# An expert down product in one fp32 pass per operand, or in three products of split operands

## The reference

```
scores = sigmoid(xt @ router_w)                 # 512 x 64, top 8 of 64 experts per token
...
def expert_block(args):                         # one block: up to 128 rows of one expert
    tok, e = args
    xb = xt[tok]                                # 128 x 1024
    h = silu(xb @ w_gate[e]) * (xb @ w_up[e])   # 128 x 256
    return h @ w_down[e]                        # 256 x 1024 weights, result 128 x 1024
...
routed = segment_sum(y * row_gate, row_tok)
```

## Time and profile before

| what | value |
|---|---|
| median of three executions | 2637.62 us (2608.13 to 2641.20) |
| the profiled execution's own time | 2625.82 us |
| its span, first to last instruction | 2623.9 us |
| busy: PE, DVE, ACT, POOL | 89%, 65%, 41%, 30% of the span |
| TensorE clock granted, mean | 0.947 of full speed |
| DMA, mean over the span | 226 GB/s |

### The profile page before, as it was taken

One profiled execution on the slowest core, in us unless ns is written; L12 is line 12 of the kernel. 1 busy time (PEld: TensorE's weight loads), 2 busy tenths in 40 slices (PEclk: granted clock), 3 DMA queues, 4 the chain that ended last, 5 costly groups with the idle time before them and its releaser, 6 DMA issues.

```text
span 2623.9 us, 35527 instructions
## 1 busy us (share of the span) xinstructions
PE 2323.8 (89%) x9437; PEld 1630.5 (62%) x9437; DVE 1695.1 (65%) x1753; ACT 1070.3 (41%) x1199; POOL 783.7 (30%) x682
## 2 busy tenths in 40 slices
PE   7652997899999999869999999798999999999995
PEld 4220455666666666647988888554666666666663
DVE  5998455666666667553257788545666666666665
ACT  2334014455555555422233333202455555555552
POOL 3663022444434434320000000002334443444432
PEclk9885989999999999988999999899999999999997
DMA  6110137999999999943232222232899999999995
GB/s 205 42 54 0 35 126 240 334 341 362 356 356 333 332 342 352 318 152 112 89 89 65 81 80 71 85 109 86 284 340 354 358 343 337 327 357 340 337 348 163
DMA packets 189297, 592.57 MB, mean 226 GB/s; under 512 B 18781, under 2 KB 88453, under 8 KB 153908
## 3 DMA queue, kind: packets, MB, share of 16 engines
q1 hardware_dynamic: 165140, 517.92, 54.1%
q0 software_dynamic: 24096, 73.88, 12.0%
HBM read 547.11 MB, written 51.38 MB: 228 GB/s over the span
## 4 chain that ended last, share of the span: by engine, by line
PE 35%; DMA 27%; DVE 12%; POOLq 11%; issue 9%; POOL 4%; ACT 1%; SPq 0%; DVEq 0%; ACTq 0%
DMA acc<-BIG,IDXS 22%; PE PS L1455 10%; POOLq L546 9%; DVE BIG L1084 6%; PE PS L1439 5%; PE PS L1237 4%; DMA BIG<-xrows,IDXG 3%; PE PS L1367 3%; PE PS L1346 3%; PE PS L1271 2%; POOL IDXS L586 2%; DMA W<-in_exp_w_up 2%; POOL IDXG L572 1%; PE PS L1468 1%; PE PS L1493 1%
## 5 line engine op out<-in xcount | busy, mean ns | idle before, releaser
L995 DVE TENSOR_TENSOR WL<-W,WH 128x2048 fp32r<-128x2048 f32 x276 | 627.9, 2291 | 276.6 <-ACT WH L691 276.0
L691 ACT ACTIVATE WH<-W 128x2048 fp32r<-128x2048 f32 x276 | 523.0, 1911 | 127.0 <-DMA W<-in_exp_w_up 118.0
L1367 PE MATMUL PS<-W,BIG 128*128 128x512 f32 x1104 | 510.6, 606 | 2.0 <-DVE BIG L1007 2.0
L1346 PE MATMUL PS<-WH,XH 128*128 128x512 f32 x1104 | 443.5, 402 | 5.8 <-DVE XL L988 5.5
L1346 PE MATMUL PS<-WH,XL 128*128 128x512 f32 x1104 | 432.2, 391 | 0.0
L1346 PE MATMUL PS<-WL,XH 128*128 128x512 f32 x1104 | 430.3, 390 | 0.0
L595 POOL DMA_INDIRECT acc<-BIG,IDXS x138 | 304.1, 2204 | 313.4 <-issue 295.3
L1367 PEld LDWEIGHTS PS<-W,BIG 128*128 128x128 f32 x1104 | 205.1, 196 | 209.3 <-issue 206.7
L1346 PEld LDWEIGHTS PS<-WH,XH 128*128 128x128 f32 x1104 | 208.1, 189 | 48.4 <-issue 8.7
L1346 PEld LDWEIGHTS PS<-WH,XL 128*128 128x128 f32 x1104 | 207.5, 188 | 45.2
L1346 PEld LDWEIGHTS PS<-WL,XH 128*128 128x128 f32 x1104 | 208.3, 189 | 39.2
(11 more groups left out here) (233 smaller groups left out, 3174.4 us busy)
## 6 DMA issues: line engine op xcount, KB each, us to landing
W<-in_exp_w_gate SPq DMA_DIRECT2D x138, 1024.0 KB, 8.1
W<-in_exp_w_up SPq DMA_DIRECT2D x138, 1024.0 KB, 11.3
W<-in_exp_w_down SPq DMA_DIRECT2D x138, 1024.0 KB, 7.0
RAW<-in_w_kv SPq DMA_DIRECT2D x48, 512.0 KB, 3.8
RAW<-in_attn_w_q SPq DMA_DIRECT2D x24, 512.0 KB, 3.7
W<-in_conv_w_in SPq DMA_DIRECT2D x8, 1024.0 KB, 11.4
acc<-BIG SPq DMA_DIRECT2D x9, 512.0 KB, 3.7
W<-in_conv_w_out SPq DMA_DIRECT2D x4, 1024.0 KB, 6.6
```

What stands on the lines that cost most here:

```text
L691: A(WH[:, s, c, :], W[:, 3 * s + c, :], ACT.Copy).then_inc(s_wh[l], 1)
L995: v.tensor_tensor(WL[s][:, c, :], W[:, 3 * s + c, :], WH[:, s, c, :].bitcast(F32), ALU.subtract).then_inc(s_wl[l], 1)
L1346: last = mm(PS[:, 3 + s, :].rearrange("p (a b) -> p a b", a=2), a, w, start=(k == 0 and i == 0), stop=(k == KT - 1 and i == 2))
L1367: last = mm(PS[:, 5 + h, :], HTm[:, s, k * P:(k + 1) * P], wd[:, k, h * 512:(h + 1) * 512], start=(k == 0), stop=(k == 1))
```

## The change

The down product is made as the gate and up products are: from a high and a low part of each operand, in three fp32r products (12 matmul calls of 512 columns per block instead of 4 float32 calls).

- ACT copies the down weights to a new buffer WDH as fp32r (`down_high(b+1)`, 128x2048), between `weights_high(b+2)` and `silu(b+1)`. It copies the transposed hidden rows to HTH (`hidden_high(b)`) at the start of its step, and it copies both halves of the output (`out(b)`).
- DVE subtracts WDH from the down slot of W in place (WDL is the same memory as W, `down_low(b+1)`, 128x2048), between `weights_low(b+2)` and `hidden(b+1)`. It makes HTL, the low part of the hidden rows, in place of its plain copy, and no longer copies any output.
- `down_proj` waits for the split weights (`s_wl`) in place of the load. SP's order and its wait for `s_yd` before a down load stay as they are.
- `s_wh` and `s_wl` now count three splits per block, and the numbers waited for follow. Two pairs of semaphores of the routing become one each, and the two for the output copies become one (the declarations, the routing and the plain renumbering are left out below). WDH and HTL lie partly over the buffer AXB, so ACT waits once per layer for the stores of `acc`.

```
                     for c in range(2):
-                        sp.wait_ge(s_wl[l], b * 2 - 3 + c)
+                        sp.wait_ge(s_wl[l], 1 + c if isinstance(b, int) and b == 2 else b * 3 - 6 + c)
                         load(3 * s + c, e)
...
                     pool.wait_ge(s_ic[l], copies)
-                    pool.wait_ge(s_ya[l], b + 1)
-                    pool.wait_ge(s_yv[l], b + 1)
+                    pool.wait_ge(s_ya[l], b * 2 + 2)
                     if not (isinstance(b, int) and b == 0):
...
                         A(WH[:, s, c, :], W[:, 3 * s + c, :], ACT.Copy).then_inc(s_wh[l], 1)
+                def down_high(b, s, it):
+                    act.wait_ge(s_mw[l][3 * s + 2], it * 16 + 16)
+                    if not (isinstance(b, int) and b < 2):
+                        act.wait_ge(s_yd[l], b - 1)
+                    A(WDH[s].rearrange("p k n -> p (k n)"), W[:, 3 * s + 2, :], ACT.Copy).then_inc(s_wh[l], 1)
+
+                def hidden_high(b, s):
+                    act.wait_ge(s_ht[l], b + 1)
+                    if not (isinstance(b, int) and b < 2):
+                        act.wait_ge(s_yd[l], b - 1)
+                    A(HTH[:, s, :], PS[:, 2, 0:F], ACT.Copy).then_inc(s_hh[l], 1)
+
                 def silu(b, s):
                     act.wait_ge(s_gu[l], b + 1)
                     A(SLm[:, s, :], PS[:, 3 + s, 0:F], ACT.Silu).then_inc(s_sl[l], 1)
-                def out_low(b, s):
+                def out(b, s):
                     act.wait_ge(s_yd[l], b + 1)
                     if not (isinstance(b, int) and b < 2):
                         act.wait_ge(s_scat[l], (b - 1) * 16)
-                    A(YB[:, s, 0:512], PS[:, 5, :], ACT.Copy).then_inc(s_ya[l], 1)
+                    for h in range(2):
+                        A(YB[:, s, h * 512:(h + 1) * 512], PS[:, 5 + h, :], ACT.Copy).then_inc(s_ya[l], 1)
                 def step(b, s, it, more):
+                    hidden_high(b, s)
                     if more:
                         weights_high(b + 2, s, it + 1)
                     if more or s == 0:
+                        down_high(b + 1, 1 - s, it + s)
                         silu(b + 1, 1 - s)
                     if more:
                         rows_high(b + 2, s)
-                    out_low(b, s)
+                    out(b, s)
                 for s in range(2):
                     rows_high(s, s)
                     weights_high(s, s, 0)
+                for k in range(2):
+                    act.wait_ge(s_acc[l][k], 16 * NT // 2)
+                down_high(0, 0, 0)
                 silu(0, 0)
                 step(0, 0, 0, True)
...
                     step(it * 2, 0, it, True)
                     step(it * 2 + 1, 1, it, True)
-                step(n * 2 - 2, 0, None, False)
-                step(n * 2 - 1, 1, None, False)
+                step(n * 2 - 2, 0, n - 1, False)
+                step(n * 2 - 1, 1, n - 1, False)
...
                                            ALU.mult, ALU.mult).then_inc(s_hd[l], 1)
-                def hidden_T(b, s):
-                    dve.wait_ge(s_ht[l], b + 1)
-                    v.tensor_copy(HTm[:, s, :], PS[:, 2, 0:F]).then_inc(s_he[l], 1)
-
-                def out_high(b, s):
-                    dve.wait_ge(s_yd[l], b + 1)
-                    if not (isinstance(b, int) and b < 2):
-                        dve.wait_ge(s_scat[l], (b - 1) * 16)
-                    v.tensor_copy(YB[:, s, 512:D], PS[:, 6, :]).then_inc(s_yv[l], 1)
+                def down_low(b, s, copies):
+                    dve.wait_ge(s_wh[l], copies)
+                    v.tensor_tensor(WDL[:, 3 * s + 2, :], W[:, 3 * s + 2, :],
+                                    WDH[s].rearrange("p k n -> p (k n)").bitcast(F32), ALU.subtract).then_inc(s_wl[l], 1)
+
+                def hidden_low(b, s):
+                    dve.wait_ge(s_hh[l], b + 1)
+                    v.tensor_tensor(HTL[:, s, :], PS[:, 2, 0:F], HTH[:, s, :].bitcast(F32), ALU.subtract).then_inc(s_he[l], 1)
                 def step(b, s, more):
-                    hidden_T(b, s)
+                    hidden_low(b, s)
                     if more:
                         weights_low(b + 2, s)
                     if more or s == 0:
+                        down_low(b + 1, 1 - s, b * 3 + 8 if more else n * 6)
                         hidden(b + 1, 1 - s)
                     if more:
                         rows_low(b + 2, s)
-                    out_high(b, s)
                 for s in range(2):
                     rows_low(s, s)
                     weights_low(s, s)
+                down_low(0, 0, 5)
                 hidden(0, 0)
                 step(0, 0, True)
...
                     last.then_inc(s_ht[l], 1)
-                def down_proj(b, s, it):
+                def down_proj(b, s, splits):
                     pe.wait_ge(s_he[l], b + 1)
-                    pe.wait_ge(s_mw[l][3 * s + 2], it * 16 + 16)
+                    pe.wait_ge(s_wl[l], splits)
                     if not (isinstance(b, int) and b == 0):
-                        pe.wait_ge(s_ya[l], b)
-                        pe.wait_ge(s_yv[l], b)
-                    wd = W[:, 3 * s + 2, :].rearrange("p (k n) -> p k n", k=2)
+                        pe.wait_ge(s_ya[l], b * 2)
+                    wdl = WDL[:, 3 * s + 2, :].rearrange("p (k n) -> p k n", k=2)
                     for h in range(2):
+                        cols = slice(h * 512, (h + 1) * 512)
                         for k in range(2):
-                            last = mm(PS[:, 5 + h, :], HTm[:, s, k * P:(k + 1) * P], wd[:, k, h * 512:(h + 1) * 512],
-                                      start=(k == 0), stop=(k == 1))
+                            hh, hl = HTH[:, s, k * P:(k + 1) * P], HTL[:, s, k * P:(k + 1) * P]
+                            wh, wl = WDH[s][:, k, cols], wdl[:, k, cols]
+                            for i, (a, w) in enumerate(((hh, wh), (hh, wl), (hl, wh))):
+                                last = mm(PS[:, 5 + h, :], a, w, start=(k == 0 and i == 0), stop=(k == 1 and i == 2))
                     last.then_inc(s_yd[l], 1)
...
                         rows_T(b + 2, s, it + 1)
-                    down_proj(b, s, it)
+                    down_proj(b, s, b * 3 + 5 if more or s == 0 else n * 6)
```

More of the change, by code:

```diff
@@ L130, in build @@
         WL = (WL0, WL1)
+        _, WDH1, HTL, _, HTH, WDH0, _, WDL = lay_out([("to_WDH1", [8192 + 10240], F32), ("WDH1", [2, D], F32R), ("HTL", [2, F], F32R),
+                                                      ("to_HTH", [20736 - 12800], F32), ("HTH", [2, F], F32R),
+                                                      ("WDH0", [2, D], F32R), ("to_WDL", [256], F32),
+                                                      ("WDL", [SLOTS, CH], F32R)])
+        WDH = (WDH0, WDH1)
         _, XTH, _, RAW, PH, PL, XTL = lay_out([("to_XTH", [NT, D], F32), ("XTH", [KT, T], F32R), ("to_RAW", [23552], F32),
@@ L187, in build @@
         Hm = big(20224, 2, F)
-        HTm = big(20736, 2, F)
         s_vec, s_posd, s_zero = sem("vec_loaded"), sem("pos_loaded"), sem("zeros_stored")
@@ L216, in build @@
         s_ob = sem("overflow_bases")
-        s_pj = [sem(f"onehots{i}") for i in range(2)]
-        s_tb = [sem(f"table_steps{i}") for i in range(2)]
+        s_pj = sem("onehots")
+        s_tb = sem("table_steps")
         s_tab = sem("tables_ready")
@@ L241, in build @@
         s_ht = [sem(f"hidden_transposed{i}") for i in range(2)]
-        s_he = [sem(f"hidden_T_copied{i}") for i in range(2)]
+        s_hh = [sem(f"hidden_T_high{i}") for i in range(2)]
+        s_he = [sem(f"hidden_T_low{i}") for i in range(2)]
         s_yd = [sem(f"expert_out{i}") for i in range(2)]
-        s_ya = [sem(f"expert_out_low_copied{i}") for i in range(2)]
-        s_yv = [sem(f"expert_out_high_copied{i}") for i in range(2)]
+        s_ya = [sem(f"expert_out_copied{i}") for i in range(2)]
         s_scat = [sem(f"scattered{i}") for i in range(2)]
@@ L945, in route @@
                     if n >= 2:
-                        dve.wait_ge(s_tb[l], n - 1)
+                        dve.wait_ge(s_tb, NT * l + n - 1)
                     s = n % 2
@@ L955, in route @@
                     v.tensor_scalar(RR[:, s, :, 0:NB], RR[:, s, :, 0:NB], pcol[:, 2 + n:3 + n], None,
-                                    ALU.mult).then_inc(s_pj[l], 1)
+                                    ALU.mult).then_inc(s_pj, 1)
                 v.tensor_scalar(tabf[0:32, 0:E], obs[0:32, 1:E + 1], pcol[0:32, 0:1], 0.0,
@@ L964, in route @@
                 v.tensor_scalar(extra[0:1, 0:1], etmp[0:1, 0:1], 1, None, ALU.logical_shift_right).then_inc(s_tab, 1)
-                dve.wait_ge(s_tb[l], NT)
+                dve.wait_ge(s_tb, NT * l + NT)
                 link(v.tensor_scalar(tabf[:, :], PS[:, 0, 256:256 + NB], 0.0, pcol[:, 1:2],
@@ L993, in weights_low @@
                     for c in range(2):
-                        dve.wait_ge(s_wh[l], b * 2 + 1 + c)
```

(7 more changed lines are left out.)

## The result

The changed kernel takes 2704.9 us (median of four, 2702.6 to 2717.7) against 2632.9 us beside it: a ratio of 1.029, 95% interval 1.024 to 1.034 (formed over the single runs; the two medians alone give 1.027, 72 us). It is slower; 2700 us was forecast.

The account below looks back on a forecast made before the run. PE (95-96% busy) and DMA (share 0.98-0.99) were both taken as near their end. A step of 11.05 + 0.25 = 11.30 us against 10.80 gives 67 us over 134 steps; with 5 + 2, 74 on 2625.8: 2700 us, range 2625 to 2800.

Parts of the forecast that it names:

- PE's term: Down product on PE: 2.93 us instead of 3.60, 0.67 us less per block, leaving PE's own step at 9.46 us.
- The reload path: Down(b-1)'s end through down load, ACT copy and DVE subtraction to PE: 15.59 us + L for two steps; 11.05 us each.
- L: Time from issue to landing of a down load: 7.0 us median, 4.8 after a long gap, taken as 6.5.
- The elementwise path: Down(b-1)'s end through ACT copies and DVE subtractions to PE's down product: 21.31 us for two steps, 10.66 a step.
- The 0.25 us on top: Added to the 11.05 us block step for gathers that still come late or a falling clock, giving 11.30 us.
- The clock rival: PE's longer waits halve its clock; one step in two adds 0.8 us a step, about 2790 us; chance 0.14.
- The faster case: PE's 0.67 us a block arrives in full in the block loops: 92 us less, 2534 us; chance 0.06.
- POOL behind DVE: Busier DVE lengthens POOL's one-column copies, so gathers start later: 0.4 us a step on top, 2750 us; chance 0.08.
- Start and ends: Loop starts, down_low(0) before hidden(0), 2.3 us twice; loop ends, last down load split alone, about 1 us twice.

Follow-up runs that it names:

- Tiny reloads: The kernel before the change, with the loop's down loads cut to 64 of 2048 columns (32 KB of 1 MB): 2537.5 us.
- both obstacles away: Changed kernel with down-weight copy and subtraction moved behind rows_high(b+2) and rows_low(b+2), and loop down loads cut to 64 columns: 2580.6 us.
- the splits behind: Changed kernel with ACT's down-weight copy moved behind rows_high(b+2) and DVE's subtraction behind rows_low(b+2): 2642.7 us, ratio 1.005 to the kernel before.

## Why the prediction came out right

- **PE's term held.** Down-product matmuls start 0.23 us apart, and the shortest steps are 9.32 us, close under the 9.46 of the sum.
- **The reload path held.** It was formed from rows of before that show no wait for a down load at all. The chain above follows it to 0.1 us, and the 99 stretches at full clock meet the longer of the two paths to 0.01 us at the median. Moving the splits out of it won 62 us; delaying its load cost 91 us, of which some 63 are L.
- **The elementwise path held as the second bound:** 10.58 us measured where 10.66 was summed. Of the 128 down loads 41 landed in under 5.7 us, so it held about a third of the stretches. Shortening it alone gave nothing.
- **L and its spread:** 6.5 us was taken, the mean of both loops is 6.4. L spreads from 4.7 to 9.8 us, and since the longer of two paths counts, that costs something by itself: taken load by load the path is 11.08 us a step, where the forecast, without a spread, had 11.05. Two small errors cancel there, by luck.
- **The 0.25 us on top held in size.** It stood for late gathers and for the clock, without saying which. Measured over the same stretches the step is 11.35 us, 0.26 above the path. Late gathers have little part in it, 1.6 us in a whole loop. The 29 half-clock phases (9 before the change) make 0.19 of it, the rest is open. The clock rival had the mechanism but far more of it, a phase in every second step and 0.8 us a step; its own sum is off too, since 134 x 0.8 is 107 and, with 0.83, 111, which on top of 2700 gives 2811 and not 2790.
- **The bound before was seen, its cause only in part.** The rows had PE at 95% and DMA at 0.98 side by side, and the prediction took DMA to be at its limit. Tiny reloads show that transfers held it; earlier gathers show that a part of that was the order on POOL and not bytes. Either way a free split could win 22 us and not 92: most of the gain was out of reach before the splits took more.
- **The faster case** failed on both of its conditions: the elementwise path takes 21.13 us for two steps, not under 20.3, and L is 6.4 us, not under 4.7. **POOL behind DVE** did not decide here, with 1.6 us of waits for gathers; with both obstacles away, gathers for which POOL was slow are what PE waits for.
- **Start and ends:** 79.7 - 71 = 9 us, where 7 were summed.

The Trainium skill (DMA: Bandwidth & Descriptors, Anatomy of one DMA — SWDGE (gpsimd) path) gives 4.4 us for 1 MB by its fit, an estimate, and the fit is for transfers that GpSimd issues, where SP issues these. The shortest landings here are 4.7 us, near it. The medians in the kernels before and after are 7.0 and 6.2 us, and with the gate and up loads issued ahead the mean rose from 6.4 to 7.4 us: other loads in the queue add to it.

## What to carry to other kernels

A load that nothing waits for is hidden by the distance to its reader. Before putting an elementwise pass between them, ask when the load starts and what is written behind the pass on the same engine; here the same instructions cost 62 us in one place of the order and almost nothing in another. Free time on an engine is worth as much as its place in the written order. And where two resources are both about 95% busy, take some of the load off one of them, and also move its transfers in time, before shortening work on the other: a DMA share of 0.98 looked like a limit of bytes and was in part one of order.

## What the runs showed that was not expected

Prefetching gathers by one more block gives 1.2% on the kernel before and costs 1.1% on the one with the splits behind. In both, ACT then waits longer for scatters; that it hurts where ACT has more to do is a guess, and no run here separates it.

And the length of PE's waits by itself does not tell when the clock falls. The half-speed `gate_up` shown above came with waits of 1.51 and 0.88 us on either side of `hidden_T`, neither as long as the 1.82 us of the earlier trace rows. In the chain of the first section waits of 1.03 and 0.88 us left the clock alone, but the two shown here, no longer, ended in a phase at half clock, with 0.54 granted from 656 to 658 us:

```profile
652.49 0.44 PE L1378 MATMUL PS<-ident,BIG 128*128 128x128 f32 x2 [0.87 <-DVE BIG L1025]
653.81 0.47 PE L1369 MATMUL PS<-WH,XH 128*128 128x512 f32 x1 [0.88 <-DVE XL L1011]
```
